# Moving a kernel's overlay region by 32 bytes in SBUF

## The reference

```python
def first_block(x, ...):                       # one layer
    h = rms_norm(x, attn_norm_w)
    r_q, r_k, r_v, r_g, c_q, c_kv, k_pe = split(h @ w_in)
    y_ret = retention_group(r_q, r_k, r_v, r_g, positions, ret_gn_w)
    y_mla = mla_group(c_q, c_kv, k_pe, positions, q_norm_w, w_uq, kv_norm_w, w_ukv)
    x = x + concat(y_ret, y_mla) @ w_out
    x = x + conv_ffn(rms_norm(x, ffn_norm_w), w_up, conv_w, conv_b, w_down)   # d_ff 2816
    return rms_norm(x, final_norm_w)

def second_block(x, c, ctx, ...):              # two layers, i = 0, 1
    for i in (0, 1):
        sh1, sc1, g1, sh2, sc2, g2 = split(silu(c) @ ada_w[i] + ada_b[i])
        y = mixer_ab(...) if i == 0 else mixer_pool(...)   # differential attention + gate, or pooling
        x = layer_norm(alpha * x + g1 * y)
        x = layer_norm(alpha * x + g2 * peer(modulate(x, sh2, sc2), wq[i], keys[i], u[i], v[i]))

def peer(h, wq, keys, u_tab, v_tab):           # 16384 experts, 8 heads, 16 of them a head
    q = h @ wq; s = q . keys                   # top 16 of each half, then top 16 of the 256 sums
    act = gelu(h . u[idx]); return sum(softmax(best) * act * v[idx])
```

## Time and profile before

| | |
|---|---|
| median of three executions | 2289.18 us (2287.78 to 2289.48) |
| the profiled execution's own time | 2289.48 us |
| its span, from the first to the last instruction | 2288.2 us |
| around the span | 1.28 us |
| mean granted TensorE clock | 0.993 of full speed |
| TensorE busy with matmuls | 2237.6 us, 98% |
| VectorE, ScalarE, GpSimd busy | 1868.9, 1199.7, 168.4 us |
| moved by DMA | 442.32 MB, mean 193 GB/s |

### The profile page before, as it was taken

One profiled execution on the slowest core, in us unless ns is written; L12 is line 12 of the kernel. 1 busy time (PEld: TensorE's weight loads), 2 busy tenths in 40 slices (PEclk: granted clock), 3 DMA queues, 4 the chain that ended last, 5 costly groups with the idle time before them and its releaser, 6 DMA issues.

```text
span 2288.2 us, 34776 instructions
## 1 busy us (share of the span) xinstructions
PE 2237.6 (98%) x13446; PEld 1887.6 (82%) x13446; DVE 1868.9 (82%) x3365; ACT 1199.7 (52%) x1754; POOL 168.4 (7%) x75
## 2 busy tenths in 40 slices
PE   9999999999999999999999999899999999999997
PEld 7789978777888888888888877788888888887886
DVE  8679996568688988888888888869998888887656
ACT  7555554456456555554444445455665554444553
POOL 0000000000044400000000000014430000000000
PEclk9999999999999999999999999999999999999999
DMA  8366593233555555555558996455555555556674
GB/s 293 123 207 218 192 356 114 92 120 102 184 176 185 188 175 169 172 170 175 175 175 300 340 357 235 147 185 185 185 185 173 173 171 173 175 175 217 218 239 136
DMA packets 123508, 442.32 MB, mean 193 GB/s; under 512 B 13760, under 2 KB 16832, under 8 KB 122704
## 3 DMA queue, kind: packets, MB, share of 16 engines
q1 hardware_dynamic: 117464, 425.04, 56.4%
q10 hardware_dynamic: 5880, 15.06, 1.9%
HBM read 436.88 MB, written 3.16 MB: 192 GB/s over the span
## 4 chain that ended last, share of the span: by engine, by line
PE 82%; DVE 10%; ACT 3%; DMA 2%; issue 2%; SPq 0%; ACTq 0%; DVEq 0%
PE psum L442 21%; PE psum L450 13%; PE psum L452 13%; PE psum L451 13%; PE psum L443 10%; PE psum L445 3%; PE psum L2864 3%; DVE low L2600 3%; DVE acc L1777 2%; PE psum L444 1%; DVE cv L2108 1%; DMA ring<-in_peer_v 1%; ACT spl L1097 1%; ACT cv L1398 1%; PE psum L918 1%
## 5 line engine op out<-in xcount | busy, mean ns | idle before, releaser
L2600 DVE TENSOR_TENSOR low<-ring,spl 128x1024 fp32r<-128x1024 f32 x638 | 779.2, 1228 | 255.0 <-ACT spl L1097 253.4
L1097 ACT ACTIVATE spl<-ring 128x1024 fp32r<-128x1024 f32 x702 | 735.4, 1053 | 288.2 <-DMA ring<-in_peer_u 163.7
L442 PE MATMUL psum<-hT,spl 128*128 128x512 f32 x2016 | 730.7, 401 | 2.5 <-DVE hT L1757 2.5
L443 PE MATMUL psum<-hT,low 128*128 128x256 f32 x2016 | 566.5, 281 | 0.0
L442 PEld LDWEIGHTS psum<-hT,spl 128*128 128x128 f32 x2016 | 381.2, 189 | 81.2 <-issue 3.1
L450 PE MATMUL psum<-spl,Ws 128*128 128x512 f32 x1024 | 407.0, 398 | 7.0 <-DVE Ws L2638 7.0
L452 PE MATMUL psum<-spl,Ws 128*128 128x512 f32 x1024 | 399.6, 390 | 0.0
L451 PE MATMUL psum<-low,Ws 128*128 128x512 f32 x1024 | 398.3, 389 | 0.0
L443 PEld LDWEIGHTS psum<-hT,low 128*128 128x128 f32 x2016 | 382.8, 190 | 9.6
L1706 ACT ACTIVATE Ws<-S 128x256 fp32r<-128x256 f32 x256 | 106.6, 417 | 357.0 <-PE psum L452 352.4
L2921 POOL TENSOR_TENSOR low<-ring,spl 128x1024 fp32r<-128x1024 f32 x64 | 162.0, 2532 | 1135.6 <-ACT spl L1097 1135.6
(11 more groups left out here) (413 smaller groups left out, 3038.1 us busy)
## 6 DMA issues: line engine op xcount, KB each, us to landing
ring<-in_peer_u SPq DMA_DIRECT2D x256, 512.0 KB, 3.5
ring<-in_peer_v SPq DMA_DIRECT2D x256, 512.0 KB, 3.7
vring<-in_ada_w SPq DMA_DIRECT2D x56, 512.0 KB, 6.2
ring<-in_w_up SPq DMA_DIRECT2D x44, 512.0 KB, 5.2
aring<-in_ada_w SPq DMA_DIRECT2D x40, 512.0 KB, 5.2
ring<-in_ab_in SPq DMA_DIRECT2D x32, 512.0 KB, 3.5
ring<-in_peer_wq SPq DMA_DIRECT2D x32, 512.0 KB, 4.3
ring<-in_w_down SPq DMA_DIRECT2D x22, 512.0 KB, 5.9
```

The lines of the kernel that those rows point to most:

```text
L442: q.matmul(b[:, :].rearrange("p (z t) -> p z t", z=2), l[0], r, start=start, stop=False)
L443: return q.matmul(b[:, 0:256], l[1], r[:, 0], start=False, stop=False)
L1097: q.activation(P.spl[:, m % SLOTS, 0:w], P.ring[:, m % SLOTS, 0:w], ACT.Copy).then_inc(*P.hi.mark(m))
L2600: q.tensor_tensor(P.low[:, n % SLOTS, 0:w], P.ring[:, n % SLOTS, 0:w], P.spl[:, n % SLOTS, 0:w].bitcast(F32), ALU.subtract).then_inc(*P.lo ...
```

## The change

`eps1` gets 8 columns in place of 16. That makes `arena` 8 words smaller and moves every overlay tile 32 bytes down; the arena then starts at byte 82528, which is 32 modulo 64 and 96 modulo 256. `cT` moves 8 words further: its word goes from 33968 to 33960, directly behind `mv`. No instruction, wait or transfer is added or removed, and no size but that of `eps1` changes.

```diff
@@ -208,7 +208,7 @@
         self.G = f("G", [128, 2, 256, 2], F16)
         self.iot16 = f("iot16", [128, 128], F16)
         self.sm = f("sm", [128, 320])
-        self.eps1 = f("eps1", [128, 16])
+        self.eps1 = f("eps1", [128, 8])
         self.arena = self.at_word
@@ -238,7 +238,7 @@
         self.mq = a("mq", 29864, [128, 2, 8, 96])
         self.mk = a("mk", 31400, [128, 2, 8, 96])
         self.mv = a("mv", 32936, [128, 2, 512])
-        self.cT = a("cT", 33968, [128, 2, 3, 256], F32R)
+        self.cT = a("cT", 33960, [128, 2, 3, 256], F32R)
         self.esb = a("esb", 29864, [128, 3, 384])
         self.rT = a("rT", 31400, [128, 2, 384])
```

## The result

The changed kernel takes 2307.76 us in the median of four executions (2306.46 to 2309.11). The kernel before takes 2289.33 in the median of four. The ratio is 1.0088, with a 95% interval of 1.0076 to 1.0100: slower by 0.9%, some 18 to 20 us. My forecast was no change, 2289.2 us, and the measured time lies above the range that I gave, 2283 to 2300.

What follows compares the result with a forecast made beforehand. TensorE, busy 98% of the span, was taken to bound the kernel; U stream, V stream, VectorE, ScalarE and transfers each added 0, giving 2289.2 us (no measurable change, 76%), range 2283 to 2300.

Steps and rivals of the forecast that it cites:

- What bounds the kernel: Whole kernel: TensorE has a matmul in flight for 98% of the span and holds 82% of the chain that ended last.
- The U part: TensorE's pairs of 512- and 256-column matmuls on fixed tiles `hT`, `spl`, `low`: 0.36 us a pair, forecast unchanged, 0 us.
- the one on weight loads: `Ws` loads in TensorE's V part: 188 ns beside matmuls 0.230 us apart, growth hidden for the first 42 ns; 0 us.
- the row of `sT`: Float32 weight loads: `sT`, at 32 modulo 64, 192 ns; `acc`, at 0, 192 ns; difference 0 ns, taken for `Ws`.
- The decision point that I named: 3072 `Ws` loads: if their cover were gone altogether, 1.5 ns a load would reach 4.6 us, the smallest difference told from none.
- the cover: V part: each `Ws` load runs beside the matmul before its own, with 42 ns to spare.
- The float16 one: Slower rival, 10%: L2864's 2048 small matmuls read `Ab` or `Bb` at 37.5 ns instead of 30; +15.4 us, 2304.6 us.
- The transfers: Slower rival, 6%: loads into the arena (`aring`, `vring`) cost more; 2293.8 us at a tenth more, about 2327 at twice.
- The faster rival: Rival, 8%: moved tiles suit some port better, as ScalarE's row 22 ns shorter at 32; 2.8 us at most, to 2286.4.
- The prediction is wrong if a price depends on the start in a form that only moved tiles have: float32r stationary operands, or float16: Refutation sign for moved tiles: an access price depending on the start address in forms without a row; no size given.
- the V stream: TensorE's six-matmul groups, 1.38 us, 0.230 us each; only stationary `Ws` moves; forecast 0 us.

Runs made afterwards that it cites:

- experiment 1: Every tile, fixed and overlay, 32 bytes up against the kernel before: 2289.03 us, ratio 0.9993.
- experiment 2: Fixed tiles 32 bytes up against the kernel before, the arena left at its byte: 2307.96 us, ratio 1.0075.
- experiment 3: Arena 64 bytes up against the kernel before (`eps1` of 32 columns): 2308.67 us, ratio 1.0082.
- experiment 7: Arena 256 bytes up against the kernel before (`eps1` of 80 columns): 2293.65 us, beside 2292.75 us for the kernel before.
- experiment 9: `hT` and the fixed tiles behind it 32 bytes up against the kernel before; ring, `low`, `spl` and arena in place: 2287.14 us, ratio 0.9986.

## Why the prediction was wrong

**What bounds the kernel** was right. TensorE sets the end: the span grew by 22.3 us and its busy time by 21.7. The U part did not move, as forecast.

**The step that failed** is the one on weight loads: the load from `Ws` "lies beside a matmul and has 230 - 188 = 42 ns to spare", with a difference of 0 ns by the row of `sT`. The load indeed did not grow, it is 188 ns in all runs. But I took its price to be its own duration. What it costs is in the duration of the stream that runs beside it, 5.5 ns of 228, and that is not hidden by anything. The decision point that I named, 1.5 ns a `Ws` matmul once the cover is gone, was passed more than three times over. I did not make a rival of it, because the cover seemed to put it beyond 42 ns.

**The variable was wrong too.** I sorted tiles by their start modulo 64 and compared rows at 0 and at 32. Experiments 1 to 3 and 7 show that neither that nor any absolute start matters, but the distance between the two tiles that TensorE reads at once, modulo 256 bytes. The rows that I trusted could not show it. `sT` is loaded beside streams of `mv`, 23552 bytes above it, and `acc` beside `ones`, 32256 bytes below it; both are multiples of 256, so that by this variable a fast row was compared with a fast row. They are of another type and shape, too, and after the change they say little: `acc` goes off its multiple, and its float32 matmuls of 128 columns repeat every 112 ns as before, while `sT` moves together with `mv`.

One row of the kernel before did show the effect, and I passed it over. `cT` begins at word 33968, 192 bytes off a multiple of 256 above `spl` and `low`, and 12 of its float32r matmuls stream 512 columns. Three of them in the timeline (start us, us, what):

```profile
37.66 0.39 PE L452 MATMUL psum<-spl,cT 128*128 128x512 f32 x1
37.88 0.39 PE L450 MATMUL psum<-spl,cT 128*128 128x512 f32 x1
38.12 0.39 PE L451 MATMUL psum<-low,cT 128*128 128x512 f32 x1
```

From one start to the next there are 225 to 236 ns, 230.5 in the mean of the eleven behind the first, against 227.7 on `Ws`. I wrote that no float32r tile lay at 32, and took 0 for such a start all the same. That was the bound to widen: 3720 matmuls (3072 on `Ws` and 648 on the other tiles) were left at zero, and 2048 float16 ones got a rival.

**The rivals.** The float16 one would have given 2304.6 us, close to the measured time, but its group did not change (193 ns, 30 ns apart); nearness of a number says nothing here. The transfers were not late. The faster rival's gain did not come from the arena, but experiment 9 shows that a shift can gain, where the streamed tile is `hT`.

**"The prediction is wrong if a price depends on the start in a form that only moved tiles have: float32r stationary operands, or float16"** was the sentence that held. The first of the two is what happened, with the distance in place of the start.

What stays open is why a multiple of 256 bytes lets the V stream settle into a steady 227 ns, and why the pairs of 512 and 256 columns prefer 16, 32 or 160 bytes. The runs show the dependence and not the circuit.

## What to carry to other kernels

Where addresses are set by hand and TensorE is busy all the time, the distance between the stationary and the streamed tile is a tuning parameter, worth 2.4% on the float32r matmuls of 512 columns (227.7 to 233.2 ns). Removing a few unused columns of a tile that lies between the two can change it; columns ahead of both move both alike, and that cost nothing (experiment 1). Price a weight load by the distance of the starts around it and not by its own duration, and widen the range where no row shows the very form (type, columns, operand) that a change touches. To find the distance, append a sweep over slices to the end of the program: one run gave 28 groups.

## What the runs showed of the hardware that I had not expected

- TensorE's stream of matmuls depends on the distance in SBUF between the tile that it streams and the one that it loads as weights beside it. With float32r, 128 stationary and 512 streamed columns: 226.7 ns at a multiple of 256 bytes, 233.3 to 233.4 at 32, 64 and 160, 228.9 at 192, 232.4 at 4 bytes. The slow groups stand in a stretch in which no other engine works.
- The loss is carried on: one slice in six that is off costs 19 ns over four matmuls.
- For the alternation of 512 (as 2 x 256) and 256 streamed columns the multiple of 256 is not the best distance: 353 ns a pair there, 347 at 16, 32 and 160 bytes, 360 at 4.
- Float32 matmuls of 128 columns with `acc` stationary do not care: 112 ns apart at a multiple of 256 bytes and 32 bytes off it. The float16 ones (30 ns) do not care where they start modulo 64; their distance was never changed, as `Ab` and `Bb` move together, and whether it counts is not shown.
